# Two hybrid blocks on one core: attention heads of block 1 turned to features by their value products, the row sums applied as diagonal matrices, and the mLSTM and compressed-attention steps moved

## The reference, cut to what matters

```python
def first_block(x, ...):
    for l in range(DEPTH):                          # DEPTH = 2
        h = rmsnorm(x, norm_mix[l])
        proj = einsum('bsd,de->bse', h, w_in[l])    # 1024 x 3476
        ...
        y_m = mlstm(...)                            # 4 heads of 128, gated recurrence
        y_b = moba(b_q, b_k, b_v, ...)              # 4 heads of 64, causal softmax
        y_n = nsa(n_q, n_kc, n_vc, n_ks, n_vs, n_kw, n_vw, n_g, ...)  # 4 heads of 64
        mix = concatenate([y_m, y_b, y_n], axis=-1)
        x = x + einsum('bse,ed->bsd', mix, w_out[l])
        h = rmsnorm(x, norm_ffn[l])
        u = square(relu(einsum('bsd,df->bsf', h, w_ff1[l])))
        x = x + einsum('bsf,fd->bsd', u, w_ff2[l])
# in nsa, with 256 tokens, for each of 4 heads and with gates g = sigmoid(g_pre):
#   o_c: softmax over 15 compressed keys, o_s and o_w: causal softmax over all keys
        return gj[:, 0] * o_c + gj[:, 1] * o_s + gj[:, 2] * o_w
```

## Time and profile before

| | us |
|---|---|
| median of 3 runs | 1129.96 (1129.31 to 1131.67) |
| the profiled execution's own time | 1128.34 |
| its span, first to last instruction | 1126.5 |
| PE busy | 1085.9 (96%) |
| DVE busy | 710.8 (63%) |
| ACT busy | 626.4 (56%) |
| POOL busy | 62.9 (6%) |
| chain that ended last | PE 76%, DVE 11%, ACT 5% |

### The profile page before, as it was taken

One profiled execution on the slowest core, in us unless ns is written; L12 is line 12 of the kernel. 1 busy time (PEld: TensorE's weight loads), 2 busy tenths in 40 slices (PEclk: granted clock), 3 DMA queues, 4 the chain that ended last, 5 costly groups with the idle time before them and its releaser, 6 DMA issues.

```text
span 1126.5 us, 17494 instructions
## 1 busy us (share of the span) xinstructions
PE 1085.9 (96%) x6848; PEld 950.1 (84%) x6848; DVE 710.8 (63%) x1203; ACT 626.4 (56%) x993; POOL 62.9 (6%) x80
## 2 busy tenths in 40 slices
PE   8999899999999999899999999999999899999997
PEld 6897779999888987789989987898988678989885
DVE  4799776556557889675555565684455657844555
ACT  4665746445445756654554444756556447566562
POOL 1010100000000100200000000004000000040000
PEclk8999999999999999999999999999999999999999
DMA  8862336665667543356666655554444446544441
GB/s 277 247 190 80 127 109 211 188 187 185 188 189 214 180 128 113 97 171 185 189 186 189 188 166 187 187 150 131 131 131 135 144 134 183 153 126 130 140 131 56
DMA packets 89087, 181.17 MB, mean 161 GB/s; under 512 B 8797, under 2 KB 19933, under 8 KB 89005
## 3 DMA queue, kind: packets, MB, share of 16 engines
q1 hardware_dynamic: 87565, 175.79, 50.6%
q10 hardware_dynamic: 1440, 4.26, 1.2%
HBM read 178.98 MB, written 1.05 MB: 160 GB/s over the span
## 4 chain that ended last, share of the span: by engine, by line
PE 76%; DVE 11%; ACT 5%; issue 5%; DMA 2%; POOL 1%; SPq 0%; DVEq 0%; POOLq 0%; ACTq 0%
PE bank L780 22%; PE bank L782 22%; PE bank L781 22%; DVE w_lo L1651 3%; ACT w_hi L1262 2%; DMA raw<-in_w_in 2%; PE bank L857 2%; PE bank L908 2%; DVE xn L1902 1%; PE bank L955 1%; PE bank L1198 1%; PE bank L964 1%; PE bank L965 1%; PE bank L931 1%; PE bank L963 1%
## 5 line engine op out<-in xcount | busy, mean ns | idle before, releaser
L1651 DVE TENSOR_TENSOR w_lo<-raw,w_hi 128x1024 fp32r<-128x1024 f32 (+1 forms) x320 | 389.7, 1221 | 300.3 <-ACT w_hi L1262 296.0
L1262 ACT ACTIVATE w_hi<-raw 128x1024 fp32r<-128x1024 f32 (+1 forms) x320 | 334.4, 1051 | 231.8 <-PE bank L782 211.2
L780 PE MATMUL bank<-h_hi,w_hi 128*128 128x256 f32 x896 | 257.4, 287 | 0.0
L782 PE MATMUL bank<-h_hi,w_lo 128*128 128x256 f32 x896 | 253.4, 283 | 0.0
L781 PE MATMUL bank<-h_lo,w_hi 128*128 128x256 f32 x896 | 253.3, 283 | 0.0
L780 PE MATMUL bank<-w_hi,h_hi 128*128 128x512 f32 (+1 forms) x448 | 182.2, 407 | 5.7 <-DVE h_lo L1670 5.1
L782 PE MATMUL bank<-w_hi,h_lo 128*128 128x512 f32 (+1 forms) x448 | 175.7, 392 | 0.0
L781 PE MATMUL bank<-w_lo,h_hi 128*128 128x512 f32 (+1 forms) x448 | 175.6, 392 | 0.0
L780 PEld LDWEIGHTS bank<-h_hi,w_hi 128*128 128x128 f32 x896 | 170.9, 191 | 3.9 <-issue 3.4
L781 PEld LDWEIGHTS bank<-h_lo,w_hi 128*128 128x128 f32 x896 | 171.0, 191 | 0.5
L782 PEld LDWEIGHTS bank<-h_hi,w_lo 128*128 128x128 f32 x896 | 170.9, 191 | 0.0
(11 more groups left out here) (290 smaller groups left out, 1297.6 us busy)
## 6 DMA issues: line engine op xcount, KB each, us to landing
raw<-in_w_in SPq DMA_DIRECT2D x144, 512.0 KB, 3.8
raw<-in_w_ff SPq DMA_DIRECT2D x128, 512.0 KB, 4.2
raw<-in_w_out SPq DMA_DIRECT2D x40, 512.0 KB, 3.3
raw<-in_w_in SPq DMA_DIRECT2D x8, 404.0 KB, 6.0
xn<-in_cmp_w SPq DMA_DIRECT2D x8, 256.0 KB, 5.2
x_sb<-in_x SPq DMA_DIRECT2D x2, 512.0 KB, 7.5
mix<-in_cmp_w SPq DMA_DIRECT2D x4, 256.0 KB, 4.5
gain<-in_cmp_w SPq DMA_DIRECT2D x4, 256.0 KB, 5.1
```

Of the source, the lines that this page charges most:

```text
L780: pe.matmul(out_ap, s_hi, m_hi, start=start, stop=False, **kw)
L782: return pe.matmul(out_ap, s_lo, m_hi, start=False, stop=stop, **kw)
L1262: act.activation(slot(w_hi, u), slot(raw, u), ACT.Copy).then_inc(hi_ready, 1)
L1651: dve.tensor_tensor(slot(w_lo, u), slot(raw, u), slot(w_hi, u).bitcast(F32), ALU.subtract)\
```

## The change

**Heads become feature-major.** The value products now use the values as the stationary operand and the transposed probabilities as the moving one. Two heads write to the two halves of the partitions of one bank (`value_pair`). The two branches of nsa accumulate in the same bank, and `cmp_o` adds the compressed branch there, so that the bank holds what `mix_turn` 2 and 3 used to make. `epilogue1`, the addition of L1953 and these two `mix_turn` steps are gone. A step `mix_rows` splits the bank directly.

**Diagonals of inverse row sums.** Since rows are no longer tokens, the division must come earlier. A new step D on DVE (`scale_rows`) takes the reciprocals of a pair's row sums, multiplies by the gates, and spreads them over four diagonal 128 x 128 matrices. T multiplies by such a diagonal in place of the transpose with the identity, as an ordinary float32 product. T waits for D (`scale_ready`).

**The order.** Pairs start at stages 13, 15, 18, 20, 22 and 24. T comes three or four stages after S in place of two or three, V five (four for the last). `probs` has four slots in block 1 and `probsT` two. The mLSTM heads have four buffers of masked scores, so all four are masked before the first `mlstm_end`. The compressed softmax is cut into `cmp_shift`, `cmp_exp` and `cmp_norm` in stages 22, 23 and 24. The eight `conv` steps end in stage 23 in place of 24.

```diff
-        start = [13, 14, 15, 16] + list(range(18, 26))
-        CONV_AT = {17 + c: (c,) for c in range(8)}
+        start = [13, 15, 18, 20, 22, 24]
+        CONV_AT = {17: (0,), 18: (1,), 19: (2,), 20: (3, 4), 21: (5,), 22: (6,), 23: (7,)}
         def heads1(p):
-            for stage, lag in (("V", 4), ("T", 2), ("E", 1), ("S", 0)):
+            for c, first in enumerate(start):
+                if first + (4 if c == 5 else 5) == p:
...
+                    step(*name, "V", 2 * c)
+                    if c in (1, 5):
+                        step("mix_rows", l, c // 4)
+            for h in range(12):
+                c = h // 2
+                if start[c] + 3 + (h % 2 if c < 5 else 0) == p:
+                    use((*name, "T", h), 4 if h == 11 else 6)
+                    step(*name, "T", h)
+            for c, first in enumerate(start):
+                if first + 2 == p:
+                    step(*name, "D", 2 * c)
+            for stage, lag in (("E", 1), ("S", 0)):
                 for h in range(12):
...
-                if p == 21:
-                    single(0, "mix_turn", 0, l, 2)
                 if p == 22:
                     single(0, "cmp_s", l, 0)
                     single(1, "cmp_s", l, 1)
-                    step("cmp_soft", l)
+                    step("cmp_shift", l)
+                if p == 23:
+                    step("cmp_exp", l)
+                if p == 24:
+                    step("cmp_norm", l)
                 if p == 27:
                     m_scores(0, 2)
                     m_scores(1, 3)
+                    m_scores(2, 5)
...
             if p == 28:
-                m_values(0, 5)
-                m_scores(2, 6)
-                m_values(1, 4)
+                m_scores(3, 4)
+                m_values(0, 6)
+                m_values(1, 5)
+            if p == 29:
                 step("mlstm_end", l, 0, 0)
-            if p == 29:
+                m_values(2, 4)
+                m_values(3, 6)
                 step("mlstm_end", l, 0, 1)
-                single(7, "mix_turn", 0, l, 3)
-                m_scores(3, 6)
-                m_values(2, 5)
-                m_values(3, 4)
             if p == 30:
                 step("mlstm_end", l, 1, 0)
-                single(6, "mix_turn", 0, l, 0)
+                step("mlstm_end", l, 1, 1)
+                single(7, "mix_turn", 0, l, 0)
             if p == 31:
-                step("mlstm_end", l, 1, 1)
                 single(5, "mix_turn", 0, l, 1)
...
+            def value_pair(l, h):
+                for c in range(2):
+                    drained(pe, ("att1", l, "T", h + c))
...
+                for i in range(NT):
+                    for c in range(2):
+                        v = heads_of("att1", l)[h + c][3](i)
+                        weight = probsT_at("att1", h + c)
+                        mm = pe.matmul(ps[HD * c:HD * c + HD, lo + i * P:lo + T], v, weight[:, i * T:i * T + T - i * P],
+                                       start=first and i == 0, stop=last and i == 1, skip_group_check=True)
...
                     for b in range(3):
-                        mm = pe.transpose(ps[:, b * P:(b + 1) * P], probs[:, h % 3, b * P:(b + 1) * P], ident)
+                        block_ = probs_at(kind, h)[:, b * P:(b + 1) * P]
+                        if kind == "att1":
+                            mm = pe.matmul(ps[:, b * P:(b + 1) * P], block_, row_scale[h // 2 % 2][:, 2 * (h % 2) + (b + 1) // 2, :],
+                                           start=True, stop=True)
...
+                def scale_rows(h):
+                    dve.wait_ge(exp_ready, nth_head("att1", l, h + 1))
+                    inv = row_inv[:, 0:2, :]
+                    link(dve.reciprocal(inv, row_sum[:, h // 2 % 2, 0:2, :]))
+                    if h >= 4:
+                        n, branch = divmod(h - 4, 4)
+                        at_gate = 4 * (1 + branch // 2) + 2 * n
+                        tt(inv, inv, n_gate[:, :, at_gate:at_gate + 2].rearrange("p i h -> p h i"), ALU.mult)
+                    dve.tensor_tensor(row_scale[h // 2 % 2], ident.unsqueeze(1).broadcast_to([P, 4, P]),
+                                      inv.rearrange("p h i -> p (h i)").unsqueeze(2).broadcast_to([P, 4, P]), ALU.mult)\
+                        .then_inc(scale_ready, 1)
```

More of the change, by code:

```diff
@@ L315, in hybrid_blocks @@
                 if p == 26:
-                    single(3, "cmp_o", l)
+                    step("cmp_o", l)
                 if p == 27:
@@ L551, in hybrid_blocks @@
         conv_in = part(2856, KD, T + 3)
-        m_probs = part(3888, 2, 384)
+        m_probs = part(2856, MH, 384)
         p_cmpT = part(4928, NT, P)
@@ L585, in hybrid_blocks @@
         prm_rows = o_tmp[:, 0:2 * P]
+        row_scale = [vecs[:, 1536 * b:1536 * b + 512].rearrange("p (n t) -> p n t", t=P) for b in range(2)]
         ident = const[:, C_ID:C_ID + P]
@@ L936, in stick_pair @@
                             close(mm, keys[c])
+            def value_pair(l, h):
+                for c in range(2):
+                    drained(pe, ("att1", l, "T", h + c))
+                group = ("att1", l, "O", h // 4 if h < 4 else 1)
+                first, last = h in (0, 4), h in (2, 10)
+                ps = open_bank(group) if first else bank[bank_of[group]]
+                lo = T * (h // 2 if h < 4 else (h - 4) // 4)
+                for i in range(NT):
[4 more added lines that the diff above has]
+                                       start=first and i == 0, stop=last and i == 1, skip_group_check=True)
+                if last:
+                    close(mm, group)
             def head_stage(kind, l, stage, h):
                 name = (kind, l)
-                if stage in ("E", "C"):
+                if stage in ("E", "C", "D"):
                     return
```

122 lines of the change are left out of this document (60 added, 62 removed).

## The result

The changed kernel took 1133.69 us, median of 6 runs (1132.84 to 1135.64), against 1129.63 us of the kernel before (1128.72 to 1131.67, 6 runs). The ratio is 1.0039, 95% interval 1.0028 to 1.0049: slower by 0.4%, where 1136.0 us and +0.5% were forecast. The profiled execution's own time is 1133.63 us, its span 1131.8, 5.3 us more than before.

A forecast was written before the change was run, and what follows sets the result against it. TensorE, busy 96% of the span, was held by late DVE and ACT answers, with DVE's queue full. Layers +4.0 and clock +2.4 gave +6.4 us on 1128.34, 1134.7; median forecast 1136 (+0.5%), range 1126 to 1144.

The forecast's parts named there:

- DVE's queue being full from 82.28 on: Stages 15 to 25: DVE last waits for TensorE at 82.28, then its queue is full until near 117.4.
- `cmp_pT`: Stage 25: its input ready at 120.8 behind DVE's queue; TensorE waits 2 us or more and is 5.0 us late.
- TensorE's own work: Per layer: T +4.0 us, V by pairs -2.9, mix_turn 2 and 3 leaving -0.9; sum +0.2, nothing.
- the 2.4 us for a clock that falls again: Both mixers: three slow stretches return, 4.8 us, half of it on time waited anyway, so +2.4 us.
- the third rival: V pairs: array halves do not work side by side with 256 moving columns; 1139 to 1144, chance 0.08.
- the 3 us per layer that I had estimated: V pairs: if each of twelve layout changes cost 0.3 us, some 3 us more per layer; not in the sum.
- silu: ACT: silu at 121.7 instead of 117.5, low part behind at 127.4 instead of 123.2; value products' wait counted unchanged.
- From `cmp_pT` to stage 32: 35.5 us before; 28.2 us of work left plus 4.3 of new waits, stage 32 starting at 153.3, 2.0 later.
- the 4.3 taken: New waits at T of head 10, mix_turn 0 and 1 and stage 32: 4.0 to 6.1 us, 4.3 taken.
- the further wait of stage 32: Stage 32 waits 0.3 to 0.5 us more, the split of mix_turn 0 being queued behind both mix_turn waits.
- one in four of twelve waits is followed by a slow stretch: Both mixers: six waits of 1.5 us or more per layer; three slow stretches come back, 4.8 us.
- The rival of no difference: New and old waits balance, at a cmp_pT wait 2 us shorter: 1130 to 1131, chance 0.15.

The follow-up runs named there:

- Experiment 1: Changed kernel without D: T multiplies by the identity and waits for the exponential alone, no division by row sums; 1130.32 us, ratio 1.0007.
- Experiment 2: Kernel before, with block 1's 12 transposes T per layer as ordinary two-pass products by the identity; 1134.38 us, ratio 1.0044.
- Experiment 9: Changed kernel with silu one stage later, in stage 26, behind the high part of unit 29; 1129.87 us, ratio 1.0004.
- experiment 6: Changed kernel with D's wide product moved to POOL, DVE keeping reciprocal and gate and handing over a copy of the factors; 1142.4 us, ratio 1.0101.
- experiment 8: Changed kernel with cmp_norm at the end of stage 23, ahead of D and row_max of heads 10 and 11; 1138.97 us, ratio 1.0074.
- experiment 3: Kernel before, with four buffers of masked mLSTM scores, all four heads masked before the first values; 1131.1 us, ratio 1.0008.
- experiment 11: Kernel before, with four buffers and mix_turn 3 ahead of the values of heads 2 and 3, mlstm_end part 1 behind them; 1122.87 us, ratio 0.9938.
- experiment 4: Kernel before, with the compressed softmax cut into three steps in stages 22, 23 and 24; 1127.87 us, ratio 0.9983.
- experiment 12: Experiment 11 with the compressed softmax in three steps, cmp_norm at the end of stage 23; 1123.27 us, ratio 0.9942.
- experiment 7: Changed kernel with mlstm_end in its earlier places, part 0 in stage 28 and part 1 of heads 2 and 3 in stage 31; 1133.23 us, ratio 1.0034.

## Why the prediction was right, and where its steps were off

**The mechanism held.** The forecast rested on DVE's queue being full from 82.28 on, so that whatever is added there reaches TensorE. DVE's last wait for scores is at 83.97 (forecast 83.6), T of head 0 waited for 1.37 us (1.5), T of head 4 started at 97.97 with 1.63 us of wait (97.6 and 1.8), `cmp_pT` at 120.83 with 1.55 us (120.8 and about 2, so late by 5.0 as forecast). Experiment 1 shows the cause: without D `cmp_pT` comes back by 4.6 us.

**The sum was right by errors that cancel.** Layer 0 can be taken apart on PE's timeline, from the last products before the paths part (65.72 before, 65.80 after) to stage 32. The wait is what the timeline lists, and the work is what is left:

| us | before | after | difference | forecast |
|---|---|---|---|---|
| waits | 8.6 | 10.8 | +2.2 | +3.4 |
| slow clock | 1.6 | 0 | -1.6 | -1.6 |
| TensorE's own work | 75.4 | 77.3 | +1.9 | +0.2 |
| sum | 85.6 | 88.2 | +2.6 | +2.0 |

The forecast of the waits is what its other terms leave of its +2.0. TensorE's own work, which I had called nothing, is nearly half of what was added. The waits are 1.2 us shorter than counted, and the 2.4 us for a clock that falls again did not come. That these three nearly cancel is luck.

**The pairs of V.** Eight matmuls of the two halves took 118.35 - 117.55 = 0.80 us (forecast 0.86), so the halves do work side by side with 256 moving columns, and the third rival is refuted. T by a diagonal took 0.67 us (123.84 to 124.51; 0.66). But the change of layout costs time outside these 0.80 us too:

```profile
123.62 0.39 PE L809 MATMUL bank<-w_hi,h_lo 128*128 128x512 f32 x1
123.84 0.83 PE L1003 MATMUL bank<-vecs,prob_store 128*128 128x128 f32 x6
...
136.72 0.40 PE L809 MATMUL bank<-w_hi,mixT_lo 128*128 128x512 f32 x1
137.04 0.87 PE L977 MATMUL bank<-prob_store,arena 128*64 128x256 f32 x8
137.84 0.70 PE L1162 MATMUL bank<-xn 128*128 128x256 f32 x2
138.38 0.38 PE L1163 MATMUL bank<-xn 128*128 128x128 f32 x2
```

From the start of a unit's last product to that of a T it is 0.22 us, to that of a V pair 0.32. The first scores of a head take 0.44 us elsewhere, and 0.54 behind a pair. With the 0.14 us by which 0.80 exceeds the 0.66 of the passes, entering and leaving cost about 0.33 us per pair, 2.0 per layer, where the sum had 0.2 per pair. The 0.61 us of the earlier trace rows, from which I called the drain small, do not contain the entry. The rule that a change of the tiling mode drains TensorE (the Trainium skill, TensorEngine Tiling (Array Packing), Key Properties) agrees with this trace: of the 3 us per layer that I had estimated by it on top of the sum, 0.8 came.

**The doubled T.** I had counted +4.0 for T and -2.9 - 0.9 for V and `mix_turn` as one sum of +0.2 us. With the 0.33 us above, V saves 2.1 and not 2.9. Experiment 2 shows that the doubled T is worth 3.0 to 4.6 us of its 8 there. What V saves was not tried alone.

**The wait that was mis-sized: silu.** The prediction said: "The value products there waited for it a little before, and I count the same wait after." Silu came at 122.29 (forecast 121.7) and the low part behind it at 127.90 (127.4), but the wait was 1.45 us in place of 0.82, plus 0.17 at T of head 10. I had the delay and not what it meets. The 0.82 us before were for `epilogue1` (L1778), another work altogether. After the change V of head 8 needs the copy of head 9's probabilities, which DVE reaches only behind that low part. Experiment 9 prices the place at 3.8 us in the changed kernel. The same move was not tried in the kernel before, whose own wait there is 0.82 us and not for silu. Experiments 1, 6 and 8 show that it is the tight place: each made DVE's earlier queue shorter or put it in another order, and each time this wait grew, to 2.4, 3.2 and 3.2 us.

**From `cmp_pT` to stage 32** I forecast 32.5 us; it took 153.95 - 120.83 = 33.1. The two `mix_turn` waited for 1.26 and 1.61 us and T of head 10 for 0.17, 3.0 in all against the 4.3 taken; the further wait of stage 32 did not come. Without the waits, the remaining work is 28.6 us (33.1 - 3.0 - 1.45) against 27.4 forecast (28.2 less the 0.82 that V waited). Of the difference, 0.3 is that `mix_turn` 1 had waited for 1.83 us in this layer and I took 2.1. Another 0.7 is side work: I let 0.5 us leave, and 0.2 came. T of head 9 ran ahead of `cmp_pT` before and runs behind it now, so three ordinary T (2.1 us) stand there in place of two transposes (0.7); V is 0.9 us shorter, and `mix_turn` 3 took 0.4. The last 0.3 is in the weight units: one that a wait follows measures 2.98 to 3.10 us with the wait taken off, the others 2.84 to 2.93, and three are followed by a wait in place of two.

**The clock** came out better than forecast: no slow stretch in either mixer of the profiled execution. The step that failed is "one in four of twelve waits is followed by a slow stretch": I had counted six waits of 1.5 us or more per layer, there are three, the longest 1.63, and over all runs only 2 of some 30 such waits were followed by one (last section). Span against span the change costs 5.3 us, within 1.3 of the layers' 4.0. Over all executions the clock loss fell by 4 to 5.5 us, where the forecast had -3.2 and +2.4. The medians are 4.1 apart, since the profiled execution before was 1.3 us under its median and the one after at its own.

**The rival of no difference** has a slip of its own: a wait of `cmp_pT` that is 2 us shorter in both layers gives 1132 by the sum, not 1130 to 1131.

**The four-buffer edit.** "Does what it says; what it frees is spent before and after it" holds: L1173 waits for nothing. But experiments 3 and 11 show a condition that I had not seen. The buffers help only where no split stands behind `mlstm_end` part 1. In the changed kernel `mix_rows` 1 stands in stage 28 and meets it; in the kernel before, `mix_turn` 3 has to be moved as well. With that the edit is worth 6.7 us alone.

**The parts together.** The exponential's unit is worth -2.0 us (experiment 4), the buffers with a free split -6.7 (experiment 11), both together -6.3 (experiment 12). The changed kernel has both and is 4.1 us slower than before. So feature-major heads with their diagonals, their later T and V and the new order of `mlstm_end` cost about 10 us in this order of work. D's queue is 3.4 of it (experiment 1), silu's place 3.8 (experiment 9), and these two overlap, since D makes silu late. TensorE's own work is up to 3.8 (1.9 per layer), `mlstm_end` 1.0 (experiment 7). How these overlap I did not take apart. The best kernel of the study is that of experiment 11.

## What to carry to other kernels

When an edit removes a wait, look on the releasing engine for what else is queued behind the same instruction: four buffers moved a wait of 3 us one step on, and moving one 0.7 us split ahead turned the same edit into a gain of 0.6%. When a stall shifts work on an in-order engine, carry the delay through to each reader of what stands behind it (here silu, then a low part, then a copy, then V); a delay that has been computed but not followed to its reader is a missing term. Work put on an engine whose queue is already late (D on DVE), or handed to a slower one (experiment 6), made this kernel slower. And where a change trades one kind of product for another, measure the passage from the product ahead to the product behind, not only the product itself: the pairs of V took 0.80 us, near the forecast, and cost 0.2 more around them.

## What the runs showed of the hardware that was not expected

POOL's time for one and the same product of 128 x 512 went from 1.04 to 1.95 us (twelve in experiment 6, the slowest at 132.92); DVE's was 0.69 each time that it is shown.

Entering and leaving the layout of two 64-wide halves costs TensorE about 0.33 us per pair: some 0.1 ahead of it, 0.14 in it and 0.1 behind (kernel after, 136.72 to 138.60).

TensorE's clock follows long waits far more often than short ones. I had put one slow stretch to four waits of 1.5 us or more. In the mixers of the two kernels and the twelve experiments, the profiled executions show: after waits of 3.0 to 3.2 us a stretch at half speed began within 1.5 us of the end of the wait in 11 of 13 cases (in five of them just before it ended), after waits of 1.8 to 2.5 us in 9 of 26, after waits of 1.5 to 1.7 us in 2 of some 30. The kernel after and experiment 9 have no mixer wait over 1.7 us and no slow stretch there. By these counts many short waits are cheaper than one long one of the same sum, by up to 1.7 us (half of 3.4) each time. No run varied the length of a wait alone, and what decides within the middle group stays open.
